# The second down projection's first 12 k tiles: seven products of block sums in place of eight products of blocks

## The reference, cut to what matters

```python
D_FF_2 = 2816
def second_block(x, ...):
    ...
    x = x + jnp.concatenate([a, p], axis=-1) @ w_out[l]
    h2 = rms_norm(x, norm2_g[l])
    x = x + (jax.nn.silu(h2 @ w_gate[l]) * (h2 @ w_up[l])) @ w_down[l]
    return x
```

## Time and profile before

| | |
|---|---|
| time, median of 3 runs | 804.93 us (804.24 to 805.11) |
| profiled execution: span | 804.6 us |
| PE, DVE, ACT, POOL busy | 797.8, 596.8, 448.1, 75.0 us |
| granted TensorE clock, mean | 0.998 of full speed |
| stage `up2` (with what leads into it), 616.0 to 741.8 us | PE 100% busy, DVE 78% |
| stage `down2`, 741.8 to 801.6 us | PE 100% busy, DVE 47% |

### The profile page before, as it was taken

One profiled execution on the slowest core, in us unless ns is written; L12 is line 12 of the kernel. 1 busy time (PEld: TensorE's weight loads), 2 busy tenths in 40 slices (PEclk: granted clock), 3 DMA queues, 4 the chain that ended last, 5 costly groups with the idle time before them and its releaser, 6 DMA issues.

```text
span 804.6 us, 13127 instructions
## 1 busy us (share of the span) xinstructions
PE 797.8 (99%) x5176; PEld 699.9 (87%) x5176; DVE 596.8 (74%) x1009; ACT 448.1 (56%) x727; POOL 75.0 (9%) x65
## 2 busy tenths in 40 slices
PE   8999999999999999999999999999999999999998
PEld 6888888999898888899999998887878888888886
DVE  6898989785555766679999996486766777778543
ACT  6577677554535544456656564366665655655431
POOL 0001000000011302101101110021100111011000
PEclk9999999999999999999999999999999999999999
DMA  9645564557442555475687665555425656656641
GB/s 316 185 158 158 166 231 147 161 145 227 122 119 89 171 173 203 162 241 177 199 247 243 216 202 196 175 186 175 142 82 170 203 176 205 196 172 208 194 151 74
DMA packets 118062, 144.09 MB, mean 179 GB/s; under 512 B 11489, under 2 KB 86641, under 8 KB 117745
## 3 DMA queue, kind: packets, MB, share of 16 engines
q1 hardware_dynamic: 115552, 141.22, 54.6%
q10 hardware_dynamic: 2448, 2.03, 1.1%
HBM read 141.78 MB, written 1.46 MB: 178 GB/s over the span
## 4 chain that ended last, share of the span: by engine, by line
PE 97%; DVE 1%; DMA 1%; ACT 0%; issue 0%; SPq 0%; DVEq 0%; ACTq 0%
PE bank L584 94%; PE bank L638 1%; DMA panel_raw<-in_w_in 1%; DVE conv_acc L1631 1%; PE bank L960 0%; PE bank L682 0%; PE bank L909 0%; DVE panel_lo L1595 0%; PE bank L933 0%; PE bank L660 0%; PE bank L737 0%; PE bank L839 0%; SPq L2400 0%; ACT panel_hi L1106 0%; DVE h L2024 0%
## 5 line engine op out<-in xcount | busy, mean ns | idle before, releaser
L1595 DVE TENSOR_TENSOR panel_lo<-panel_raw,panel_hi 128x1024 fp32r<-128x1024 f32 x245 | 308.0, 1259 | 138.9 <-ACT panel_hi L1106 138.5
L584 PE MATMUL bank<-x_halves,panel_hi 128*128 128x256 f32 (+1 forms) x1536 | 368.3, 322 | 0.7 <-DVE x_halves L2031 0.7
L1106 ACT ACTIVATE panel_hi<-panel_raw 128x1024 fp32r<-128x1024 f32 (+1 forms) x247 | 260.4, 1055 | 176.6 <-PE bank L584 174.6
L584 PE MATMUL bank<-x_halves,panel_lo 128*128 128x256 f32 x1024 | 289.1, 282 | 0.0
L584 PEld LDWEIGHTS bank<-x_halves,panel_hi 128*128 128x128 f32 x1536 | 257.0, 191 | 23.3 <-issue 0.9
L584 PEld LDWEIGHTS bank<-x_halves,panel_lo 128*128 128x128 f32 x1024 | 195.7, 191 | 0.2
L584 PE MATMUL bank<-panel_hi,x_halves 128*128 128x512 f32 x384 | 122.0, 399 | 0.0
L584 PEld LDWEIGHTS bank<-panel_hi,x_halves 128*128 128x128 f32 x384 | 70.0, 188 | 14.4 <-DVE panel_lo L1595 0.6
L584 PE MATMUL bank<-panel_lo,x_halves 128*128 128x512 f32 x192 | 75.1, 391 | 0.0
L584 PE MATMUL bank<-panel_hi,act_hi 128*128 128x512 f32 x176 | 68.6, 390 | 0.0
L584 PE MATMUL bank<-panel_hi,act_lo 128*128 128x512 f32 x176 | 68.5, 389 | 0.0
(11 more groups left out here) (291 smaller groups left out, 913.1 us busy)
## 6 DMA issues: line engine op xcount, KB each, us to landing
panel_raw<-in_w_in SPq DMA_DIRECT2D x35, 1024.0 KB, 5.3
panel_raw<-in_w_up SPq DMA_DIRECT2D x30, 1024.0 KB, 5.2
panel_raw<-in_w_down SPq DMA_DIRECT2D x20, 1024.0 KB, 5.0
panel_raw<-in_w_gate SPq DMA_DIRECT2D x10, 1024.0 KB, 5.3
panel_raw<-in_w_out SPq DMA_DIRECT2D x8, 1024.0 KB, 5.1
panel_raw<-in_w_in SPq DMA_DIRECT2D x11, 512.0 KB, 5.5
panel_raw<-in_w_branch_fox SPq DMA_DIRECT2D x4, 1024.0 KB, 5.0
panel_raw<-in_w_branch_gdn SPq DMA_DIRECT2D x4, 1024.0 KB, 5.1
```

What stands on the lines that cost most here:

```text
L584: return e.matmul(o, l, r, start=start, stop=stop, skip_group_check=True)
L1106: return e.activation(o, i_, ACT.Copy, scale=scale)
L1595: e.tensor_tensor(lo, raw_view(i, k0, kt), hi.bitcast(F32), ALU.subtract).then_inc(s_lo, 1)
```

## The change

The first 12 k tiles of `w_down` are taken in 3 groups of 4 k tiles. In a group, the even k tiles form block row 1 and the odd ones block row 2; with the two column halves this gives four blocks b11, b12, b21, b22 of 128 x 1024 numbers, each the size of a half panel. Instead of multiplying each block with both token tiles (8 block products, each of 2 k tiles x 3 = 6 matmuls), seven products are formed. The weights of four of them are sums: t3 = b12 + b22, t2 = t3 + b11, t1 = b11 + b12, t4 = t2 + b21. They pair with activations of one tile (b11, b21, t4) or with sums and differences of activation tiles (t1, t2, t3, b22). The product of each kind runs into a bank of its own over all groups (b11, t1, t2 and t3 into banks that `down2` did not use), and eight DVE operations (`block_sums`), with one copy on ACT, combine them into `h`.

- The weight sums are made by transfers: GpSimd issues a transfer from HBM that adds the second block to what lies in the buffer of the first (`add_block`, `accum_op`). t3, t2 and t4 are made one out of the other in the buffer of b12, t1 in that of b11. Each add but a group's first waits until the sum before it in its buffer has been split. The split of a sum waits for its add.
- The activation sums are three additions on GpSimd for each of j = 0 to 5 (`act2_sums`), split by one more copy on ACT and one more subtraction on DVE.
- The blocks of groups 0 and 1 are loaded during `up2`, those of group 2 into the buffers of group 0 when these are free.
- The other 10 k tiles keep the old product in 10 half panels ("plain" steps), which stand among the block products. `down2` has 31 steps: 21 block products of 6 matmuls and 10 plain steps of 12.

By number, with a dash for a plain step: **1** t3, **2** b11, **3** -, **4** b21, **5** b22, **6** t2, **7** -, **8** t1, **9** -, **10** t4; group 1 the same in steps **11** to **20**; group 2: **21** t3, **22** b11, **23** -, **24** b21, **25** b22, **26** t2, **27** t1, **28** -, **29** t4, **30** -, **31** -.

```diff
+GROUPS = 3
+DOWN2_ORDER = [(12, 0), (12, 1), (16, 0), (20, 0), (16, 1), (20, 1)]
+BLOCKS = ("b11", "b12", "b21", "b22")
...
+GROUP_ORDER = [("t3", "b11", None, "b21", "b22", "t2", None, "t1", None, "t4")] * (GROUPS - 1) \
+    + [("t3", "b11", None, "b21", "b22", "t2", "t1", None, "t4", None, None)]
+BLOCK_BANK = {"b11": ("p1",), "b21": ("down2", 0, 0), "b22": ("down2", 1, 0), "t4": ("down2", 0, 1), "t1": ("p5",),
+              "t2": ("p6",), "t3": ("p7",)}
...
+BLOCKS_FROM = [END["up2", 1, 4], END["up2", 1, 6], BLOCK_AT[0, "t4"] - 2]
+SUMS_FROM = [BLOCKS_FROM[0] + 6, BLOCKS_FROM[1] + 6, BLOCK_AT[1, "t3"]]
...
+            def block_product(n):
+                _, g, b = HALVES[n - 1]
+                hi, lo = (panel_view(w[(n - 1) % 4], "wide", 0, 2) for w in (whi, wlo))
+                o, first, last = down2_bank(n, BLOCK_BANK[b])
+                e.wait_ge(s_lo, n)
+                for k in range(2):
...
+                    for m, (xx, ww) in enumerate(((xh, hi), (xl, hi), (xh, lo))):
+                        i_ = mm(o, xx, ww[:, k, :], first and k == 0 and m == 0, last and k == 1 and m == 2)
+                i_.then_inc(s_half, 1)
...
                 i, k0, kt = HALVES[n - 1]
+                if i is None:
+                    g, b = k0, kt
+                    e.wait_ge(*block_ready(g, b))
+                    e.wait_ge(s_half, n - 4)
+                    copy(whi[(n - 1) % 4], block_raw[g % 2][KEPT_IN[b]]).then_inc(s_hi, 1)
+                    return
...
+                if n == TOUCHES["p1",][-1]:
+                    e.wait_ge(s_block_sums, 1)
+                    copy(sum_u, bank_of(("p1",))).then_inc(s_u_copied, 1)
...
+            def block_sums(n):
+                if n == TOUCHES["p1",][-1]:
+                    e.wait_ge(s_half, n)
+                    e.wait_ge(s_half_rsq, 1)
+                    add_to_rows(0, 0, bank_of(("p1",))).then_inc(s_block_sums, 1)
+                if n == TOUCHES["p6",][-1]:
+                    e.wait_ge(s_half, n)
+                    e.wait_ge(s_u_copied, 1)
+                    e.tensor_tensor(sum_u, bank_of(("p6",)), sum_u, ALU.add).then_inc(s_block_sums, 1)
+                    e.wait_ge(s_block_sums, 2)
+                    e.tensor_tensor(sum_v, bank_of(("p7",)), sum_u, ALU.add).then_inc(s_block_sums, 1)
+                if n == TOUCHES["p5",][-1]:
+                    e.wait_ge(s_half, n)
+                    e.tensor_tensor(minus_w, bank_of(("p5",)), sum_u, ALU.subtract).then_inc(s_block_sums, 1)
+                    e.wait_ge(s_block_sums, 3)
+                    e.tensor_tensor(p5_less_v, bank_of(("p5",)), sum_v, ALU.subtract).then_inc(s_block_sums, 1)
+                if n == TOUCHES["p5",][-1] + 1:
+                    e.wait_ge(s_block_sums, 5)
+                    add_to_rows(1, 0, minus_w).then_inc(s_block_sums, 1)
+                    add_to_rows(0, 1, sum_v).then_inc(s_block_sums, 1)
+                    add_to_rows(1, 1, p5_less_v).then_inc(s_block_sums, 1)
...
+            def act2_sums(j):
...
+                e.wait_ge(s_g_mul, j + 1)
+                e.tensor_tensor(s_[:, SUM_3:SUM_1 + 1, :], x_[:, 0:2, :], x_[:, 1:4:2, :], ALU.subtract).then_inc(s_sums, 1)
+                e.wait_ge(s_sums, 3 * j + 1)
+                e.tensor_tensor(s_[:, SUM_2, :], s_[:, SUM_1, :], x_[:, 0, :], ALU.subtract).then_inc(s_sums, 1)
+                e.wait_ge(s_sums, 3 * j + 2)
+                e.tensor_tensor(s_[:, SUM_4, :], x_[:, 2, :], s_[:, SUM_2, :], ALU.add).then_inc(s_sums, 1)
+
+            def add_block(g, b, src, after, split=True):
+                buf = KEPT_IN[b]
+                e.wait_ge(*block_ready(g, after))
+                if split:
+                    e.wait_ge(*block_split(g, after))
+                e.dma_start(block_view(block_raw[g % 2][buf]), block_rows(g, src), accum_op=ALU.add) \
+                    .then_inc(s_block_add[g % 2][buf], 16)
...
+                for g in range(GROUPS):
+                    if n == SUMS_FROM[g]:
+                        add_block(g, "t3", "b22", "b12", False)
+                    if n == BLOCK_AT[g, "t3"] - 2:
+                        add_block(g, "t2", "b11", "t3")
+                    if n == BLOCK_AT[g, "b11"] - 2:
+                        add_block(g, "t1", "b12", "b11")
+                    if n == BLOCK_AT[g, "t2"] - 2:
+                        add_block(g, "t4", "b21", "t2")
```

More of the change, by code:

```diff
@@ L141, in panels @@
             out.append((("up2", s, j), "norm2", "hl", w, 0, KD, j * PW, PW))
-    for k, c in DOWN_ORDER:
+    for k, c in DOWN2_ORDER:
         add_wide(("down2", c), "act2", "w_down_2", k, min(HALF, KF - k), c * WIDE)
@@ L150, with with_blocks @@
           for k in range(0, p[5], n)]
+def with_blocks(halves):
+    plain = [x for x in halves if PLAN[x[0]][0][0] != "down2"]
+    down2 = iter(halves[len(plain):])
+    return plain + [next(down2) if b is None else (None, g, b) for g, order in enumerate(GROUP_ORDER) for b in order] \
+        + list(down2)
+HALVES = with_blocks(HALVES)
+BLOCK_AT = {(g, b): n + 1 for n, (i, g, b) in enumerate(HALVES) if i is None}
 EARLY = (4, 5, 6)
@@ L586, in tensor_program, with x_ready_for, down2_bank, down2_first @@
             waited = set()
+            def x_ready_for(x, kx):
+                if (x, kx // 2) not in waited:
+                    waited.add((x, kx // 2))
+                    e.wait_ge(*x_ready(x, kx))
+            def down2_bank(n, key):
+                if n == TOUCHES[key][0]:
+                    for s, v in room(key):
+                        e.wait_ge(s, v)
+                return bank_of(key), n == TOUCHES[key][0], n == TOUCHES[key][-1]
+            def down2_first():
+                for key in DOWN2_BANKS:
+                    bank_for("side" if len(key) == 1 else "gemm", key)
@@ new lines, in down2_product @@
+            def down2_product(n):
+                i, k0, kt = HALVES[n - 1]
+                (_, c), x, how, _, kp, _, _, _ = PLAN[i]
+                hi, lo = (panel_view(w[(n - 1) % 4], how, 0, kt) for w in (whi, wlo))
+                e.wait_ge(s_lo, n)
+                for j in range(TT):
+                    o, first, last = down2_bank(n, ("down2", c, j))
+                    js = slice(j * P, (j + 1) * P)
+                    for k in range(kt):
+                        kx = kp + k0 + k
+                        x_ready_for(x, kx)
+                        for m, (xx, ww) in enumerate(((acth, hi), (actl, hi), (acth, lo))):
+                            i_ = mm(o, xx[:, kx, js], ww[:, k, :], first and k == 0 and m == 0,
+                                    last and k == kt - 1 and m == 2)
+                    if last and j == 0:
+                        i_.then_inc(will_fill(("down2", c, 0)), 1)
+                i_.then_inc(s_half, 1)
@@ L588, in gemm @@
             def gemm(n):
                 i, k0, kt = HALVES[n - 1]
+                if n == END["up2", 1, KF // 2 - 1] + 1:
+                    down2_first()
+                if i is None:
+                    block_product(n)
+                    return
+                if PLAN[i][0][0] == "down2":
+                    down2_product(n)
+                    return
                 key, x, how, _, kp, _, _, _ = PLAN[i]
@@ L2413, in sync_program @@
                         fetch(i)
+                for g in range(GROUPS):
+                    for at_, b in zip(range(0, 8, 2) if g < 2 else (0, 0, 0, 0), ("b12", "b11", "b21", "b22")):
+                        if n == BLOCKS_FROM[g] + at_:
+                            if g < 2:
+                                e.wait_ge(*emptied(("out2", 1, 1)))
+                            else:
+                                e.wait_ge(*block_split(g - 2, {"b11": "t1", "b12": "t4"}.get(b, b)))
+                            e.dma_start(block_view(block_raw[g % 2][b]), block_rows(g, b)).then_inc(block_landed(g, b)[0], 16)
                 if n == 3:
```

87 lines of the change are left out of this document (81 added, 6 removed).

## The result

The changed kernel takes **811.97 us** (median of 4 runs, 811.65 to 813.91), the kernel before, beside it, 804.66 (804.24 to 805.11): a ratio of 1.0094, interval 1.0081 to 1.0107. It is 0.9% slower, where I had forecast 802.8 and a small gain; the time lies at the upper end of the range, 0.03 us inside it. What happened is the rival "the chain of adds sets PE's pace".

The account below looks back on a forecast made before the run. PE, busy for 99% of the span, was taken as the bound: 4.08 us of matmuls removed, less waits of L - 3.6 and 1.24 us, gave a gain of 2.2 us off 804.93, 802.8 us; range 801.2 to 812.0.

Parts of the forecast that it names:

- the chain of adds sets PE's pace: Rival in `down2`: ACT's order links five adds, stage longer than 59.88 us from L = 6.4, 808 us at 7; chance 0.27.
- What is removed: Step on `down2`: 18 matmuls go at 0.2268 us each, 4.08 us; the stage falls from 59.88 to 55.80 us.
- What `up2` gets: Step on `up2`: 1.98 us of GpSimd sums per j, DVE at 9.16 of 11.09 us; no time lost.
- What an add costs: Step on `down2`'s adding transfers: 4.25 us each from issue to landing, 3.5 to 8.5 kept as possible.
- L: Time of one adding transfer of 512 KB from issue to landing, taken as 4.25 us.
- Where an add is late: Step on `down2`: only group 2's t4 is late, PE waits L - 3.6, then 1.24 us at step 30; gain 2.2 us.
- 53.4 + L: Length of `down2` with the late last t4 and the wait at step 30; 57.7 us at L = 4.25.
- the end of the kernel: Column half 1's sums and the writes, behind the last matmul: claimed to stay as before, no time added.
- Adds in time: Claim on `down2`'s other adds: t2 and t4 of a group lie 8.16 us apart, against L + 2.35 = 6.6.
- 28 + 5L: Length of `down2` if five adds in a row set the pace; each us of L beyond 6.4 costs five.

Follow-up runs that it names:

- run 1: Changed kernel without all twelve adding transfers, so the weight sums are missing from the output: 800.92 us, 0.9951 of the kernel before.
- run 4: Changed kernel without the 18 GpSimd sums of activations; ACT and DVE split the product itself at the same sizes: 812.35 us, 1.0096 of the kernel before.
- run 5: Changed kernel without the four plain loads of group 2's blocks; all waits and adds stay: 809.71 us, 1.0062 of the kernel before.
- run 2: Changed kernel with its twelve GpSimd transfers overwriting their target instead of adding, 512 KB each: 803.75 us, 0.9990 of the kernel before.
- run 8: Changed kernel's three groups run beside each other as far as possible, the third in four buffers of its own: 802.36 us, 0.9969 of the kernel before.
- runs 2 and 3: Run 2 as in its own line; run 3: changed kernel, each add moving 256 KB instead of 512: 803.80 us, 0.9992 of the kernel before.
- run 7: The two groups of run 6 run beside each other instead: 802.12 us, 0.9971 of the kernel before; repeated unchanged, 801.87 us.
- run 6: Changed kernel with two groups instead of three, same order within a group, k tiles 8 and up plain: 809.88 us, 1.0062 of the kernel before.

## Why the prediction was wrong

**What is removed: right.** 18 x 0.2268 = 4.08 us; run 1 shows 59.66 - 55.58 = 4.08.

**What `up2` gets: right in the time, wrong in the size.** GpSimd's three sums of one j:

```profile
659.18 1.00 POOL L2526 TENSOR_TENSOR act_sums<-f_tanh 128x256 f32<-128x256 f32 x1
660.26 1.33 POOL L2528 TENSOR_TENSOR act_sums<-act_sums,f_tanh 128x128 f32<-128x128 f32 x1
661.67 1.33 POOL L2530 TENSOR_TENSOR act_sums<-f_tanh,act_sums 128x128 f32<-128x128 f32 x1
```

3.66 us, where I took 1.98 from the additions of the earlier trace rows. DVE's load is 9.99 of 11 us, not 9.16 of 11.09. It stays under PE's, and run 4 shows that nothing of it reaches the time. The rule that I had set against this edit (the Trainium skill, SBUF — State Buffer, section Who interferes with whom), that a DVE instruction with two SBUF inputs contends with a GpSimd instruction that reads SBUF, agrees with the trace: DVE is 1.07 us a cycle longer beside the sums.

**What an add costs: this step failed.** I took L = 4.25, half way between 3.5 and 5.0, with the second reading "partly beside the first". It isn't beside it: an add alone took 5.6 to 5.9 us (changed kernel, run 5), 1.7 to 2.0 more than the plain transfer of run 2 with 3.9, where I had put 0.75 on top of 3.5. And L is not one number. In company it was 7.2 in the median and 10.1 where it counted, since I had asked how long an add takes and not how many transfers stand beside it. The fit that I had cited (the Trainium skill, DMA: Bandwidth & Descriptors, section Anatomy of one DMA — SWDGE (gpsimd) path) gives 3.2 us for 512 KB; run 2 measures 3.9 to 4.1 without adding, and the measurement decides. The section SWDGE vs HWDGE vs iDMA of the same page of the Trainium skill says that only one queue for GpSimd's transfers is allocated. The landings of run 8, one after another, are what one queue would give, but with a DMA share of 1.11 full engines give it too, and no run here tells the two apart.

**Where an add is late: right, as a formula, but for the end.** For the late t4 alone I had 53.4 + L for the stage. Run 2 had L = 3.91 at that place, which gives 57.3; it measured 57.51 to the last start and 57.74 to its end. What I had missed is the end of the kernel. I let it stay as it is; but DVE, late by that wait, does the three row additions of the sums behind the last splits:

```profile
803.40 2.08 DVE L2044 SCALAR_TENSOR_TENSOR h<-block_sum,stats,h 128x512 f32<-128x512 f32 x3
805.58 2.07 DVE L2084 SCALAR_TENSOR_TENSOR h<-bank,stats,h 128x512 f32<-128x512 f32 x3
```

In the earlier trace rows two of the four last additions are done at 794.7, 7 us before the last matmul; here all of them follow 803.4. That is the 0.94 us, in runs 2 and 3 too, and not in run 1.

**"Adds in time": wrong.** I counted 8.16 us between t2 and t4 of a group against L + 2.35, and so held only the last add to be late. With the L that they had, ACT waited for seven adds, 22.5 us in all, in every group, and its order hands the delay on to the next group's t3.

**The chain of adds: the rival that came true**, with 28 + 5L for the stage. The five adds took 6.10 + 10.11 + 6.53 + 6.41 + 5.85 = 35.0 us. To this come 0.49 us four times between the split and GpSimd's issue, and 2.84 us once (744.71 to 747.55, where the last product of `up2` stood ahead of the add on GpSimd), 4.8 in all, which I had not counted; and the first link began 4.26 us after the stage's start (744.71 - 740.45), not 5.9. 28 - 1.64 + 35.0 + 4.8 = 66.2 us; measured are 66.11 + 0.23 = 66.34. I gave this 0.27, because the panels of `w_down` land in 5.0; they add nothing to what is there. That the time lies inside the range is luck: at the measured mean of 35.0 / 5 = 7.0 us my chain gave 808, and the upper end of 812.0 stood on an L of 7.8. The rest are the 4.8 - 1.64 = 3.2 us of hand-overs and the 0.94 us at the end that I had at nothing.

## What to carry to other kernels

Price a transfer that adds at twice its bytes, and ask how many transfers stand beside it: here 5.6 to 5.9 us alone and, where five adds stood together (run 8), 3 to 4 us more for each one ahead. A chain of such transfers is hidden by order, not by speed: two chains beside each other made 2.5 us of gain (run 7) out of 5.2 of loss (run 6) with the same instructions. And an engine that takes its work in order hands a late operand on to work that was ready, here t4 of one group to t3 of the next.

## What the runs showed of the hardware

- An adding transfer of 512 KB from GpSimd: 5.6 to 5.9 us alone, with 1.19 us of GpSimd for its issue; plain from GpSimd 3.9 and 0.72; an add of 256 KB 4.1 and 0.86.
- Five adds issued within 7 us landed 2.9 to 4.1 us apart at a DMA share of 1.11 (run 8); one took 10.1 us beside four plain loads, two adds and a panel, and 5.6 without the four loads (run 5).
- After 3.68 us without a matmul the granted clock was 0.50 for about 3 us, and matmuls 0.43 us apart; after 1.63 us (run 8) they were 0.23 apart from the second on.
- A GpSimd addition of 128 x 128 took 1.33 us here, one of 128 x 256 1.00; the trace of before had 0.58 for 128 x 128.
